# Writing only the normalised value ahead of a modulation, and folding scale and bias into its columns

## What is computed

```python
h = x * (1.0 + sc1) + sh1                       # modulation 1
y = mix_latent(project_heads(h, ...), ...)
x = layer_norm(ALPHA * x + g1 * y, ln1_g, ln1_b)
h = x * (1.0 + sc2) + sh2                       # modulation 2
y = expert_choice_ffn(h, w_router, w_gate, w_up, w_down)
x = layer_norm(ALPHA * x + g2 * y, ln2_g, ln2_b)

def layer_norm(x, g, b):
    mu, var = x.mean(-1), ((x - mu) ** 2).mean(-1)
    return (x - mu) * rsqrt(var + LN_EPS) * g + b
```

## Time and profile before

| | |
|---|---|
| time, median of 3 runs | 1745.07 us (1743.33 to 1748.67) |
| profiled execution: span from first to last instruction | 1743.7 us |
| what lies around the span, taken as median minus span | 1.4 us |
| PE busy | 1512.4 us (87%) |
| DVE busy | 507.1 us (29%) |
| ACT busy | 400.2 us (23%) |
| bytes moved | 522.71 MB, mean 300 GB/s |

### The profile page before, as it was taken

How to read it: one execution, slowest core, us unless ns; L and a number is a source line. 1 busy time by engine, 2 the same in 40 slices (tenths; PEclk the granted TensorE clock), 3 DMA queues, 4 the chain that set the end, 5 groups by cost and what they waited for, 6 DMA issues and landing times.

```text
span 1743.7 us, 23509 instructions
## 1 busy us (share of the span) xinstructions
PE 1512.4 (87%) x9968; PEld 832.1 (48%) x9968; DVE 507.1 (29%) x1002; ACT 400.2 (23%) x860; POOL 23.2 (1%) x47
## 2 busy tenths in 40 slices
PE   7999998999999998899888899899997667676764
PEld 3544346888885343433222375578863233332322
DVE  0243666434552000011010365765620000000003
ACT  1222676222321010200000142854320001000000
POOL 1000000000000000000000100000000000000000
PEclk9999999999999999999999999999997788877767
DMA  9644932323558999999999931056989999999995
GB/s 367 243 177 198 420 111 64 113 81 112 193 220 310 422 421 421 421 420 421 422 421 421 330 112 49 1 174 194 361 360 420 421 421 421 421 420 421 421 421 223
DMA packets 101510, 522.71 MB, mean 300 GB/s; under 512 B 11024, under 2 KB 13344, under 8 KB 47136
## 3 DMA queue, kind: packets, MB, share of 16 engines
q1 hardware_dynamic: 97712, 509.97, 73.3%
q0 software_dynamic: 3392, 10.85, 1.9%
q10 hardware_dynamic: 304, 0.40, 0.1%
HBM read 520.04 MB, written 1.15 MB: 299 GB/s over the span
## 4 chain that ended last, share of the span: by engine, by line
PE 58%; SPq 21%; DMA 14%; DVE 4%; ACT 1%; issue 1%; DVEq 0%; ACTq 0%
PE psum L533 54%; SPq L1121 21%; DMA ring<-in_w_down 7%; DMA ring<-in_w_up 5%; PE psum L618 4%; DMA A<-in_w_down 2%; DMA ring<-in_w_ada 1%; DVE X L1881 1%; ACT hT L1267 0%; DVE X L1774 0%; DVE X L1775 0%; DVE small L1744 0%; DVE PR L1763 0%; DVE small L1749 0%; DVE stats L1887 0%
## 5 line engine op out<-in xcount | busy, mean ns | idle before, releaser
L533 PE MATMUL psum<-ring,A 128*32 128x256 f32 (+1 forms) x1920 | 278.5, 548 | 76.2 <-DMA ring<-in_w_up 41.5
L533 PE MATMUL psum<-ring_r,h_hi 128*128 128x512 f32 x704 | 219.7, 394 | 6.9 <-DVE h_lo L1781 5.8
L533 PE MATMUL psum<-A 128*32 128x256 f32 (+5 forms) x1152 | 182.8, 534 | 33.9 <-DMA A<-in_w_up 17.8
L533 PEld LDWEIGHTS psum<-ring,A 128*32 128x32 f32 (+1 forms) x1920 | 89.1, 137 | 251.1 <-issue 105.7
L1915 DVE TENSOR_TENSOR W<-W,psum 128x512 f32<-128x512 f32 (+1 forms) x32 | 17.8, 555 | 542.0 <-PE psum L533 542.0
L533 PE MATMUL psum<-ring,PR 128*32 128x256 f32 (+1 forms) x1080 | 142.7, 493 | 36.8 <-DMA ring<-in_w_down 36.7
L533 PE MATMUL psum<-ring,hT 128*128 128x512 f32 (+3 forms) x512 | 162.9, 471 | 3.4 <-issue 1.3
L533 PE MATMUL psum<-ring_r,h_lo 128*128 128x512 f32 x384 | 150.7, 392 | 0.0
L533 PEld LDWEIGHTS psum<-ring_r,h_hi 128*128 128x128 f32 x704 | 133.1, 190 | 35.5 <-issue 6.6
L533 PEld LDWEIGHTS psum<-A 128*32 128x32 f32 (+3 forms) x1152 | 60.6, 143 | 123.8 <-issue 57.8
L533 PEld LDWEIGHTS psum<-ring,hT 128*128 128x128 f32 x512 | 85.1, 192 | 69.2 <-issue 66.9
(11 more groups left out here) (204 smaller groups left out, 1449.1 us busy)
## 6 DMA issues: line engine op xcount, KB each, us to landing
ring<-in_w_down SPq DMA_DIRECT2D x93, 1024.0 KB, 25.6
ring<-in_w_up SPq DMA_DIRECT2D x85, 1024.0 KB, 25.3
ring<-in_w_gate SPq DMA_DIRECT2D x80, 1024.0 KB, 25.3
ring<-in_w_ada SPq DMA_DIRECT2D x40, 1024.0 KB, 14.6
A<-in_w_up SPq DMA_DIRECT2D x40, 1024.0 KB, 26.0
A<-in_w_gate SPq DMA_DIRECT2D x38, 1024.0 KB, 26.3
ring<-in_w_in SPq DMA_DIRECT2D x36, 1024.0 KB, 5.2
A<-in_w_down SPq DMA_DIRECT2D x28, 1024.0 KB, 26.1
```

Source lines behind the costliest of these rows:

```text
L533: return nc.tensor.matmul(o, a, b, start=start, stop=stop, skip_group_check=True)
```

## The change

- Every norm that a modulation follows (the first norm of both layers and the second of layer 0) now writes `(x - mean) * rstd` in one pass (`standardize`). The last norm of the kernel stays as it was.
- `behind_norm` folds scale and bias of the norm into the modulation columns: shift += scale * b, then scale *= g. It is called three times, in `ada_columns`. For this, six rows of norm parameters are loaded as 8 x 128 blocks by six more POOL transfers, PE transposes them once and DVE copies them to `norm_cols`.
- The true value is restored later by `scaled`, in two passes over a tile: at expert 7 together with `ALPHA`, where one pass stood, and in layer 1's projection in new steps "X" of DVE for tiles 2 and 3.
- `norm_par` for the second norm is issued after `raised`, that is after expert 7's restoring, instead of at the end of the routing.
- ACT takes the next tile's root between the two halves of a modulation instead of behind both.

```diff
+DVE_NEXT = [("P", 1, 0), ("P", 1, 1), ("P", 3, 0), ("P", 3, 1), ("U", 0), ("P", 2, 0), ("U", 1), ("X", 2), ("U", 2),
+            ("X", 3)] + QKV_STEPS[18:]
...
+            pe.wait_ge(norm_rows_in, 96)
+            transposes("norm", [norm_rows], bank=TURN_BANK)
...
+                if l == 0:
+                    for i, v in enumerate((ln1_g[0, :], ln1_b[0, :], ln1_g[1, :], ln1_b[1, :], ln2_g[0, :],
+                                           ln2_b[0, :])):
+                        pool.dma_start(norm_rows[KT * i:KT * i + KT, :], v.rearrange("(k p) -> k p", p=P)) \
+                            .then_inc(norm_rows_in, 16)
...
-                norm_par(l, False)
+                norm_par(l, ln1_g, ln1_b)
+                gate_rows(l)
 
                 pool.wait_ge(x_ready, 2 * first_tile(l) + len(tiles(l)))
-                norm_par(l, True)
+                gate_y_rows(l)
                 if l == 0:
                     store_rows(1)
+                pool.wait_ge(raised, l + 1)
+                norm_par(l, ln2_g, ln2_b)
...
-                    modulated("h2T", l, t, SC2, SH2, (0, 1) if i < len(ts) - 1 else (0,))
+                    modulated("h2T", l, t, SC2, SH2, (0,))
                     if i < len(ts) - 1:
                         norm_root(2 * first_tile(l) + i + 2)
+                        modulated("h2T", l, t, SC2, SH2, (1,))
...
+            def behind_norm(scale, shift, g, b):
+
+                more = small[:, 80:96].rearrange("p (s k) -> p s k", s=2)
+                g, b = (v.unsqueeze(1).to_broadcast([P, 2, KT]) for v in (g, b))
+                run(V_.tensor_tensor(more, scale, b, ALU.mult))
+                run(V_.tensor_tensor(shift, shift, more, ALU.add))
+                run(V_.tensor_tensor(scale, scale, g, ALU.mult))
...
+                    if kind == "X":
+                        filled(dve, ("hT", l, t, 1))
+                        scaled(t, 1.0)
...
+            def standardize(n, t):
+
+                moments(n, t)
+                run(V_.tensor_scalar(X[:, t, :], X[:, t, :], small[:, 41:42], small[:, 46:47], ALU.subtract, ALU.mult))
+                mark(x_ready)
+
+            def scaled(t, factor):
+
+                run(V_.scalar_tensor_tensor(X[:, t, :], X[:, t, :], factor, norm_g, ALU.mult, ALU.mult))
+                run(V_.scalar_tensor_tensor(X[:, t, :], norm_b, factor, X[:, t, :], ALU.mult, ALU.add))
...
                         for t in tiles(l):
-                            run(V_.tensor_scalar(X[:, t, :], X[:, t, :], ALPHA, None, ALU.mult))
+                            scaled(t, ALPHA)
+                        mark(raised)
...
-                dve.wait_ge(norm_par_in, 160 * l + 160)
+                dve.wait_ge(norm_par_in, 160 * l + 128)
...
+                dve.wait_ge(norm_par_in, 160 * l + 160)
                 scatter(4)
```

More of the change, by code:

```diff
@@ L208, in trunk @@
         bias_rows, cin = part(A, 0, P)[0:48 * DEPTH, :], part(A, 128, P)[0:2 * KT, :]
+        norm_rows = part(A, 256, P)[0:6 * KT, :]
+        norm1_of, norm2_first = {l: (norm_cols[:, 2 * l, :], norm_cols[:, 2 * l + 1, :]) for l in range(DEPTH)}, \
+            (norm_cols[:, 4, :], norm_cols[:, 5, :])
         norm_g, norm_b = part(PR, 0, D), part(PR, D, D)
@@ L617, in transposes @@
                 for i, s in enumerate(sources):
-                    ins = nc.tensor.transpose(psum[0:rows, b, i * P:(i + 1) * P], s, ident)
+                    n = s.shape[0]
+                    ins = nc.tensor.transpose(psum[0:rows, b, i * P:i * P + n], s, ident[0:n, 0:n])
                 end(ins, b)
@@ L1165, in row, with norm_par, gate_rows, gate_y_rows @@
                 return ap.rearrange("(a n) -> a n", a=1).partition_broadcast(P)
-            def norm_par(l, second):
-                g, b = ((ln2_g, ln2_b) if second else (ln1_g, ln1_b))
+            def norm_par(l, g, b):
                 pool.dma_start(norm_g, row(g[l, :])).then_inc(norm_par_in, 16)
                 pool.dma_start(norm_b, row(b[l, :])).then_inc(norm_par_in, 16)
[L1172 to L1176, removed]
+            def gate_rows(l):
+                for s in (0, 1):
+                    pool.dma_start(gate_of[s], row(mod_all[l, s, 8 * G1:8 * G1 + 8, :].rearrange("c p -> (c p)"))) \
+                        .then_inc(norm_par_in, 16)
+            def gate_y_rows(l):
                 w = D * CAP * len(streams(l)) // P
@@ L1773, in layer_norm @@
                 run(V_.reciprocal(small[:, 46:47], small[:, 43:44]))
[L1774 to L1775 removed]
+            def standardize(n, t):
[5 more added lines that the diff above has]
+                run(V_.scalar_tensor_tensor(X[:, t, :], norm_b, factor, X[:, t, :], ALU.mult, ALU.add))
+            def layer_norm(n, t):
+                moments(n, t)
+                run(V_.scalar_tensor_tensor(X[:, t, :], X[:, t, :], small[:, 41:42], norm_g, ALU.subtract, ALU.mult))
+                run(V_.scalar_tensor_tensor(X[:, t, :], X[:, t, :], small[:, 46:47], norm_b, ALU.mult, ALU.add))
                 mark(x_ready)
@@ L1837, in route @@
                     residual(l, t, 1)
-                    layer_norm(l, t, 2 * first_tile(l) + i, X[:, t, :])
+                    standardize(2 * first_tile(l) + i, t)
                 modulated("h2T", l, tiles(l)[-1], SC2, SH2)
@@ L1887, in normalized @@
                         run(V_.bn_stats(stats[:, t, n, :], X[:, t, 512 * n:512 * n + 512]))
-                    layer_norm(l, t, 2 * first_tile(l) + len(tiles(l)) + i, X[:, t, :])
+                    norm = standardize if l < DEPTH - 1 else layer_norm
+                    norm(2 * first_tile(l) + len(tiles(l)) + i, t)
                 def scatter(g):
@@ L1940, in _ @@
                 modulated("hT", 0, t, SC1, SH1)
+            b = filled(dve, "norm")
+            V_.tensor_copy(norm_cols[:, :, :], psum[:, b, 0:6 * KT].rearrange("p (i k) -> p i k", k=KT)) \
+                .then_inc(bank_drained[b], 1)
+            drained(dve, "norm")
             step = QKV_TURNS
             for l in range(DEPTH):
-                qkv(l, DVE_FIRST + QKV_NEXT if l else QKV_STEPS)
+                qkv(l, DVE_FIRST + DVE_NEXT if l else QKV_STEPS)
                 dve.wait_ge(sink_in, 16 * (l + 1))
```

11 lines of the change are left out of this document (8 added, 3 removed).

## The result

The changed kernel takes 1755.34 us (median of 4 runs, 1754.77 to 1759.11) where the kernel before took 1744.40 beside it: a ratio of 1.0059, 95% interval 1.0045 to 1.0074. It is slower, by 10 to 11 us. Its profiled span is 1752.9 us, the number that the sum gave, but that is partly luck, as the stages will show.

What follows compares the result with a forecast made beforehand. Bound: DMA bytes inside the two expert plateaus, PE's chain outside. Terms 0.15 + 0.2 + 0.3 + 5.0 - 0.25 + 3.4 + 0.4 = +9.2 on span 1743.7 gave 1752.9, plus 1.4: 1754.3 us; range 1745 to 1759.

Steps and rivals of the forecast that it cites:

- the two large terms: Second-norm loads in both layers' expert stages, +5.0 us, and two restoring steps in layer 1's projection, +3.4 us.
- rival of one large term hidden: A later wait hides the 3.4 us (1750.9) or slack in the expert stages hides the loads (1749.3); chance 0.18.
- rival of a faster kernel: The normalisations lie on PE's path after all, at most -9 us, 1736; chance 0.12.
- slower rival: Stalls in layer 1's projection reach later steps, or TensorE's clock falls after the new waits: 1760; chance 0.06.
- Loads in the plateau: Second-norm rows, 1.05 MB a layer, load while experts keep DMA full: +2.49 us a layer, +5.0 in all.
- Steps X: Layer 1's projection: DVE's restoring of tiles 2 and 3 makes PE wait 1.3 and 2.1 us, +3.4 in all.
- Second norm: Layer 0's second norm, ahead of layer 1's projection: PE's wait of 0.26 us goes, throw-away passes stay, -0.25 us.
- Columns: Three calls folding scale and bias on DVE in layer 0's attention, where PE mostly leads: +0.2 us.
- start: Kernel start: one more PE transpose and a copy, +0.15 us.
- First norm of layer 0: Layer 0's routing: PE gains about 0.4 us from shorter normalisation, ACT's order costs 0.7; net +0.3 us.
- First norm of layer 1: Layer 1's routing: ACT's second half comes one root later, 0.3 to 0.4 us, delaying PE: +0.4 us.
- the faster rival's last tiles: Last tile of each of three norms, where throw-away passes end near DVE's signal: some 3 us if PE's clock rises.

Runs made afterwards that it cites:

- after_short_warm: The changed kernel with fewer thrown-away matmuls (2 in place of 7, 14 in place of 20): 1749.67 us, 1.0021 of the kernel before.
- rows_last: Changed kernel, restoring steps later, matmuls cut, ACT's old order, second-norm rows loaded in layer 1's projection and behind the last expert's last product: 1740.69 us, 0.9975.

## Why the prediction was right, and where its terms were off

The direction, the two large terms and their places held. The time of 1754.3 lies 1.0 us from the median. Part of that is the term for what lies around the span: I had 1.4 us, and all four runs of the changed kernel have 1.8. The rival of one large term hidden fell with the two kernels that undo or isolate a term; the rival of a faster kernel fell with the waits for the normalised tiles, which weren't in the rows. Of the slower rival the clock's fall came in one trace of two, but not through the new waits.

- **Loads in the plateau, 2.49 a layer.** The steps in SP's queue measure 2.4 to 2.7, and the loads alone give 1.0036. The rule of the Trainium skill that I weighed (DMA: Bandwidth & Descriptors, "Issuing engines are not separate DMA queues") holds here: the loads of POOL delay those of SP by their full bytes, 5.1 us in two layers where queues of their own would have given 0. Around the steps the expert stages vary by up to 2 us more: at the head of the first plateau by -0.2 to +1.9 us, and in the last weights by 0 to +2.3, in kernels with and without the loads. What makes that I haven't found.
- **Steps X, 3.4.** 3.06: a pass with an immediate takes 1.22 us, not the 1.285 of one with a column scalar, and four of them make most of the difference.
- **Second norm, -0.25.** -0.48. The wait of 0.26 went, and the start of PE's next transposes won 0.2 us that no row had as a wait.
- **Columns, +0.2; start, +0.15.** 0.05 and 0.38. PE led DVE in the attention throughout; the transpose row itself lasts 0.26 us, twice what I took from a group of eight.
- **First norm of layer 0, +0.3.** -0.18 and +0.19. In the first trace that is 0.93 us won at the first two tiles, where I had put 0.4, against the wait of 0.75 us for ACT.
- **First norm of layer 1, +0.4.** This is the term that failed: 1.6 us in both traces. The step was "ACT's second half comes one root later, 0.3 to 0.4". The order costs some 0.9 by the undone order, and a second stretch at half clock 0.8.
- **Clock.** The sum had no term for it outside the ends. In the first trace a fall in layer 1's attention cost 1.7 us, which I first laid on the X steps; the runs took that back. It and the 1.2 us too much in layer 1's routing are as large as the chance gain at the start, -1.99, and the smaller misses together, and only so did the span come out at 1752.9.
- **What the normalisation is worth.** I put the faster rival's last tiles at 3 us in all. With the cover cut they gave 8 us by stages, of which up to 2.5 can be the clock's, and 7 by time: not only is each tile ready earlier, the thrown-away passes themselves, at 0.24 us each in the half-clock places, are off the path.

## What to carry to other kernels

Shortening an engine's work pays nothing while filler work stands in front of the one who waits for it: cut the filler together with the wait, and check the old kernel with the same cut, to see what each is worth. In a stage that is full of transfers, every byte added costs its time, and moving a small load out of a moment that looks busy into one that is busy is a loss; the free moments are where the queue is empty, and they can be read from the windows. New work on an engine belongs where it waits anyway: two steps of 2.5 us cost 3.06 us at one place in the list and nothing five steps further. And before 1 or 2 us in one stage are laid on an edit, the same kernel should be traced a second time.

## What the runs showed of the hardware

- DVE's pass over 128 x 1,024 values: 1.285 us with two tensors and a column scalar, 1.22 us with two tensors and an immediate, 0.81 us with one tensor and two column scalars, and 0.694 us with one tensor and an immediate. So one column scalar costs 0.06 us more than an immediate with two tensors, and two cost 0.12 more with one tensor.
- TensorE's clock falls at the same places in some executions and not in others. The first scores of layer 1's attention took 1.95 or 1.96 us in half of the fourteen traces and 2.67 to 3.75 in the other half, and the changed kernel alone had one of each. The product behind that attention has a stretch at half in eleven of the traces and none in three, and again the changed kernel had one of each. Such a stretch costs up to 1.7 us of PE, and a longer one in the first scores cost 3.4 (`after_short_warm`, `rows_last`), so one trace can't lay 1.7 us on an edit. What sorts them stays open: a kernel that was never run twice may have its outcome by its timing.
- The first product of 16 matmuls lasted 7.10 and 10.13 us in two executions of one kernel. It moves all that follows: at 32 us the traces lie between 2.1 us ahead of the kernel before and 2.1 behind. It isn't the weights: in the kernel before they have landed at 20.21, and the product begins at 23.26. PE's weight loads in that product, early and late in it:

```profile
24.25 0.33 PEld L533 LDWEIGHTS psum<-ring,hT 128*128 128x128 f32 x1 [0.52 <-issue]
...
27.90 0.19 PEld L533 LDWEIGHTS psum<-ring,hT 128*128 128x128 f32 x1 [0.24 <-issue]
```

A matmul with its load takes 0.85 us at first (0.33 + 0.52) and 0.43 later, half of it. The traces with a product of 7.10 us have no slow ones, and that of 10.13 has seven. So PE went from one pace to twice that pace at another point of the product in each execution; the granted clock in the windows reads 1.00 throughout here, so that this was the clock is argued from the paces alone.
